# Hymba-style step on one core: first norm from token rows, x turned block by block, weight units at the head of the first pass

## What is computed

```
mod = (silu(c) @ ada_w + ada_b)             # 9 vectors of 2048 for each of 9 conditions
h = rmsnorm(x, g1) * (1 + sc1) + sh1        # rmsnorm: x * rsqrt(mean(x*x) + eps) * g
x = x + 0.5 * gt1 * (silu(h @ wg) * (h @ wu)) @ wd      # 2048 -> 5504 -> 2048
...                                         # mixer, second feed-forward, last norm
```

## Time and profile before

| | us |
|---|---|
| median of 3 runs | 2408.03 |
| lowest, highest | 2407.75, 2410.68 |
| the profiled execution | 2407.99 |
| its span, first to last instruction | 2405.5 |
| PE busy in the span | 2356.3 (98%) |
| DVE busy | 1202.7 (50%) |
| ACT busy | 838.0 (35%) |
| POOL busy | 151.1 (6%) |

### The profile page before, as it was taken

The page is one execution under the profiler, slowest core; times in us unless marked ns, Lnnn a source line. Parts: engine busy times, 40 slices in busy tenths (PEclk is TensorE's granted clock), DMA queues, the critical chain, the costliest instruction groups (busy, mean ns, idle before and its releaser), DMA issues.

```text
span 2405.5 us, 45693 instructions
## 1 busy us (share of the span) xinstructions
PE 2356.3 (98%) x17264; PEld 2258.3 (94%) x17264; DVE 1202.7 (50%) x2084; ACT 838.0 (35%) x1130; POOL 151.1 (6%) x176
## 2 busy tenths in 40 slices
PE   7999999999999999998999998999999999999998
PEld 3888999999999999998999898999999999999998
DVE  3665434434533454357676746454454454456344
ACT  3332222222222232334566634332333232333234
POOL 3000000000000000021031211000000000000003
PEclk9999999999999999999999999999999999999999
DMA  9999998889889948863444453554554555454553
GB/s 316 359 332 350 281 278 266 263 262 278 270 258 278 270 147 245 255 192 114 146 134 123 123 148 116 147 157 138 154 157 140 149 156 148 140 159 147 145 154 104
DMA packets 680252, 480.98 MB, mean 200 GB/s; under 512 B 15349, under 2 KB 603785, under 8 KB 679801
## 3 DMA queue, kind: packets, MB, share of 16 engines
q1 hardware_dynamic: 678224, 473.36, 65.8%
q0 software_dynamic: 1776, 6.26, 0.8%
q10 hardware_dynamic: 162, 0.14, 0.0%
HBM read 476.53 MB, written 5.13 MB: 200 GB/s over the span
## 4 chain that ended last, share of the span: by engine, by line
PE 91%; DVE 4%; ACT 2%; issue 1%; DMA 1%; DVEq 0%; ACTq 0%
PE ps L558 28%; PE ps L560 28%; PE ps L559 28%; PE ps L569 6%; PE ps L544 1%; DVE lo L1366 1%; DMA ident<-in_identity 0%; ACT hi L1021 0%; DMA mod_raw<-in_ada_w 0%; DVE work L1679 0%; DVE h_lo L1412 0%; DVE work L1725 0%; DVE work L1681 0%; DVE work L1401 0%; DVE work L1427 0%
## 5 line engine op out<-in xcount | busy, mean ns | idle before, releaser
L558 PE MATMUL ps<-h_hi,hi 128*128 128x320 f32 x3456 | 1079.0, 312 | 18.5 <-DVE h_lo L1412 11.8
L560 PE MATMUL ps<-h_hi,lo 128*128 128x320 f32 x3456 | 1070.5, 310 | 0.0
L559 PE MATMUL ps<-h_lo,hi 128*128 128x320 f32 x3456 | 1070.5, 310 | 0.0
L1366 DVE TENSOR_TENSOR lo<-raw,hi 128x1024 fp32r<-128x1024 f32 (+1 forms) x608 | 731.8, 1221 | 492.3 <-ACT hi L1021 491.1
L1021 ACT ACTIVATE hi<-raw 128x1024 fp32r<-128x1024 f32 (+1 forms) x608 | 624.9, 1050 | 1009.6 <-PE ps L560 875.9
L558 PEld LDWEIGHTS ps<-h_hi,hi 128*128 128x128 f32 x3456 | 651.3, 188 | 35.2 <-issue 28.4
L559 PEld LDWEIGHTS ps<-h_lo,hi 128*128 128x128 f32 x3456 | 651.4, 188 | 0.7
L560 PEld LDWEIGHTS ps<-h_hi,lo 128*128 128x128 f32 x3456 | 651.2, 188 | 0.0
L558 PE MATMUL ps<-a_hi,hi 128*128 128x320 f32 x1376 | 426.8, 310 | 1.3 <-DVE a_lo L1540 1.3
L560 PE MATMUL ps<-a_hi,lo 128*128 128x320 f32 x1376 | 425.2, 309 | 0.0
L559 PE MATMUL ps<-a_lo,hi 128*128 128x320 f32 x1376 | 425.1, 309 | 0.0
(11 more groups left out here) (221 smaller groups left out, 875.5 us busy)
## 6 DMA issues: line engine op xcount, KB each, us to landing
raw<-in_ffn_w_gate SPq DMA_DIRECT2D x172, 512.0 KB, 4.2
raw<-in_ffn_w_up SPq DMA_DIRECT2D x172, 512.0 KB, 5.1
raw<-in_ffn_w_down SPq DMA_DIRECT2D x160, 512.0 KB, 4.8
mod_raw<-in_ada_w SPq DMA_DIRECT2D x144, 512.0 KB, 7.8
work<-in_ada_w SPq DMA_DIRECT2D x144, 512.0 KB, 8.2
raw<-in_w_in SPq DMA_DIRECT2D x56, 512.0 KB, 3.8
raw<-in_w_out SPq DMA_DIRECT2D x32, 512.0 KB, 3.8
raw<-in_ffn_w_down SPq DMA_DIRECT2D x16, 384.0 KB, 2.9
```

Of the source, the lines that this page charges most:

```text
L558: mm(out, w_hi, r_hi, start=first, stop=False)
L559: mm(out, w_hi, r_lo, start=False, stop=False)
L560: return mm(out, w_lo, r_hi, start=False, stop=last)
L1366: v.tensor_tensor(lo_slot(u)[:, 0:n], raw_slot(u)[:, 0:n], hi_slot(u)[:, 0:n], ALU.subtract).then_inc(lo_done, 1)
```

## The change

It has four parts.

1. **First norm token by token.** The squares of the first norm are no longer taken from the turned blocks. ACT squares the three token tiles with a sum along the row (`accum_out`), makes rstd for each token by Ln and Exp on a 128x3 tile, DVE multiplies the identity by each of the three columns (`diag`), and PE multiplies ones by these three diagonals (`spread_rstd`), which lays rstd along the row on all partitions; ACT copies it out. POOL's 16 additions, the 16 squares on ACT and the sum by ones are gone; POOL's sample work for the first norm multiplies by rstd first, then by scale, then adds the shift.
2. **x turned one block per modulation unit.** Two blocks ahead, then one after each of the first 14 of the 16 units of groups 0 and 1. The parameters are turned after the seventh, `mod_turn(0)` after the ninth, `spread_rstd` after the tenth.
3. **Weight units first.** In the first quarter PE's order becomes unit 0, unit 1, group 2 parts 0 to 3, unit 2, unit 3, group 2 parts 4 to 7, unit 4, `mod_turn(2)`, unit 5, group 3 (all eight), unit 6, `mod_turn(3)`, unit 7. SP's order becomes units 0, 1, group 2 parts 0 to 3, units 2, 3, group 2 parts 4 to 7, units 4, 5, group 3 (all eight), units 6 to 9, group 4 parts 0 to 3, units 10, 11, and on.
4. **The identity first** in ACT's queue of transfers, ahead of c.

```
+TURN_AT = 2
+HALVES_0 = {2: ((2, 0),), 4: ((2, 4),), 6: ((3, 0), (3, 4))}
...
-            for u in range(4):
+            for u in range(8):
+                for group, first in HALVES_0.get(u, ()):
+                    head_group(group, range(first, first + 4))
                 head_unit(u)
-            head_group(2, range(MODS))
-            for u in range(4, 8):
+            for u in range(8, 10):
                 head_unit(u)
...
+            for h in range(4, 22):
+                head_group(2 + h // 2, range(h % 2 * 4, h % 2 * 4 + 4))
+                head_unit(2 * h + 2)
+                head_unit(2 * h + 3)
...
+            def spread_rstd():
+                pe.wait_ge(diag_ready, 1)
+                for t in range(3):
+                    n = P if t < 2 else SAMP
+                    last = mm(psum[:, 5, t * P:t * P + n], ones[0:n, :], diag[0:n, t, 0:n], start=True, stop=True)
+                last.then_inc(rstd_spread, 1)
 
             pe.wait_ge(x_in, 3 * 16)
+            for k in range(TURN_AT):
+                turn_x(k)
+            pe.wait_ge(c_ready, 1)
             for u in range(FIRST):
-                if u < MODS:
-                    turn_x(2 * u)
-                    turn_x(2 * u + 1)
-                if u == 0:
-                    pe.wait_ge(c_ready, 1)
                 mod_unit(u % MODS, u // MODS)
-                if u == MODS - 1:
+                if u + TURN_AT < KB:
+                    turn_x(u + TURN_AT)
+                if u == MODS - 2:
                     turn_parameters()
+                if u == MODS:
                     pe.wait_ge(prm_ready, 1)
                     mod_turn(0)
-                if u == SUM_AT:
-                    sum_of_squares(0)
+                if u == MODS + 1:
+                    spread_rstd()
             mod_turn(1)
...
                 for i in range(8):
-                    if i % 2 == 0:
+                    if q == 0:
+                        halves = HALVES_0.get(i, ())
+                    else:
+                        halves = ((first if i < 4 else second, i % 4 * 2),) if i % 2 == 0 else ()
+                    for group, part in halves:
                         for n in range(4):
-                            mod_unit(i % 4 * 2 + n, first if i < 4 else second)
+                            mod_unit(part + n, group)
                     quarter_unit(q, i)
-                    if i == 2:
+                    if i == (4 if q == 0 else 2):
                         mod_turn(first)
...
+            act.dma_start(ident[:, :], io['identity']).then_inc(ident_in, 16)
             act.dma_start(c_tok[0:1, :], io['c_prompt']).then_inc(c_in, 16)
             act.dma_start(c_tok[1:NC_, :], io['c_sample']).then_inc(c_in, 16)
-            act.dma_start(ident[:, :], io['identity']).then_inc(ident_in, 16)
...
-            for k in range(KB):
-                square(k, 0, dve_freed, k + 1)
+            act.wait_ge(x_in, 3 * 16)
+            squares = h_hi[:, :, :].rearrange("p k n -> p (k n)")
+            more = h_lo[:, :, :].rearrange("p k n -> p (k n)")
+            for t in range(2):
+                run(squares[:, t * D:(t + 1) * D], x_tok[:, t, :], ACT.Square, accum_out=ssq[:, t:t + 1])
+            chain(run(more[0:SAMP, 0:D], x_tok[0:SAMP, 2, :], ACT.Square, accum_out=ssq[0:SAMP, 2:3]))
+            chain(run(ssq, ssq, ACT.Ln, bias=eps, scale=1.0 / D))
+            run(ssq, ssq, ACT.Exp, scale=-0.5).then_inc(first_rstd, 1)
             copy_group(0)
+            act.wait_ge(rstd_spread, 1)
+            run(rstd, psum[:, 5, 0:T], ACT.Copy).then_inc(rstd_ready, 1)
             split(0)
...
-                    if i == 2:
+                    if i == (4 if q == 0 else 2):
                         copy_group(2 * q + 2)
...
-            parameters()
-            add_mod(0, 0)
+                if k == 7:
+                    parameters()
+                if k == 9:
+                    add_mod(0, 0)
+                    dve.wait_ge(first_rstd, 1)
+                    v.tensor_scalar(diag[:, 0, :], ident[:, :], ssq[:, 0:1], None, ALU.mult)
...
-            add_squares(0, KB)
-            samples(1, 0)
+            first_samples()
```

More of the change, by code:

```diff
@@ L101 @@
 SIDE_BY_SIDE = ((0, 0), (1, 0), (0, 1), (1, 1))
-SUM_AT = MODS + 1
-SUMMED = (0, KB, 2 * KB - 1, 3 * KB - 2)
-SET_UP = 2
+TURN_AT = 2
+HALVES_0 = {2: ((2, 0),), 4: ((2, 4),), 6: ((3, 0), (3, 4))}
+SUMMED = (0, 0, KB - 1, 2 * KB - 2)
+SET_UP = 3
 def mixer_plan():
@@ L216, in build @@
         sum_sq, at = carve(at, T)
+        diag, _ = carve(at - T, 3, P)
         sq, at = carve(at, 2, T)
@@ L280, in build @@
         sink_pick = small[:, 74:78]
+        ssq = small[:, 42:45]
         eps = small[:, 78:79]
@@ L477, in _ @@
             head_group(1, range(MODS))
-            for u in range(4):
+            for u in range(8):
+                for group, first in HALVES_0.get(u, ()):
+                    head_group(group, range(first, first + 4))
                 head_unit(u)
-            head_group(2, range(MODS))
-            for u in range(4, 8):
+            for u in range(8, 10):
                 head_unit(u)
[L483 to L492, removed]
+            for h in range(4, 22):
+                head_group(2 + h // 2, range(h % 2 * 4, h % 2 * 4 + 4))
+                head_unit(2 * h + 2)
+                head_unit(2 * h + 3)
+            for u in range(46, 48):
+                head_unit(u)
             head_group(13, range(MODS))
@@ L602, in sum_of_squares @@
             def sum_of_squares(n):
[L603 to L610, removed]
+                pe.wait_ge(summed, SUMMED[n] + KB - 1)
+                mm(psum[:, B_NORM, 0:T], ones, sum_sq, start=True, stop=False)
+                pe.wait_ge(squared, n * KB)
+                mm(psum[:, B_NORM, 0:T], ones, sq[:, (KB - 1) % 2, :], start=False, stop=True).then_inc(ms_ready, 1)
+            def spread_rstd():
[4 more added lines that the diff above has]
+                last.then_inc(rstd_spread, 1)
             pe.wait_ge(x_in, 3 * 16)
+            for k in range(TURN_AT):
+                turn_x(k)
+            pe.wait_ge(c_ready, 1)
             for u in range(FIRST):
-                if u < MODS:
-                    turn_x(2 * u)
-                    turn_x(2 * u + 1)
-                if u == 0:
-                    pe.wait_ge(c_ready, 1)
                 mod_unit(u % MODS, u // MODS)
-                if u == MODS - 1:
+                if u + TURN_AT < KB:
+                    turn_x(u + TURN_AT)
+                if u == MODS - 2:
                     turn_parameters()
+                if u == MODS:
                     pe.wait_ge(prm_ready, 1)
                     mod_turn(0)
-                if u == SUM_AT:
-                    sum_of_squares(0)
+                if u == MODS + 1:
+                    spread_rstd()
             mod_turn(1)
@@ L997, in _ @@
             token_sums(sum_sq, B_NORM)
-            pe.wait_ge(squared, 3 * KB + KB)
+            pe.wait_ge(squared, 3 * KB)
             token_sums(sq[:, (KB - 1) % 2, :], B_LAST)
@@ L1062, in copy_group @@
                 copy_mod()
-            for k in range(KB):
-                square(k, 0, dve_freed, k + 1)
+            act.wait_ge(x_in, 3 * 16)
[6 more added lines that the diff above has]
+            run(ssq, ssq, ACT.Exp, scale=-0.5).then_inc(first_rstd, 1)
             copy_group(0)
+            act.wait_ge(rstd_spread, 1)
+            run(rstd, psum[:, 5, 0:T], ACT.Copy).then_inc(rstd_ready, 1)
             split(0)
-            run(warm, eps, ACT.Ln)
-            act.wait_ge(ms_ready, 1)
-            chain(run(ln_ms, psum[:, B_NORM, 0:T], ACT.Ln, bias=eps, scale=1.0 / D))
             copy_group(1)
-            run(rstd, ln_ms, ACT.Exp, scale=-0.5).then_inc(rstd_ready, 1)
             modulate(0, 0, 0, Q)
@@ L1849, in _ @@
             g.memset(eps, EPS).then_inc(set_up, 1)
+            g.memset(ssq, 1.0).then_inc(set_up, 1)
             row = 0
@@ L1884, in add_squares @@
                 for m in range(end):
-                    pool.wait_ge(squared, n * KB + m + 1)
+                    pool.wait_ge(squared, (n - 1) * KB + m + 1)
                     if m == 0:
-                        if n:
-                            pool.wait_ge(ms_ready, n)
+                        if n > 1:
+                            pool.wait_ge(ms_ready, n - 1)
                         g.tensor_copy(sum_sq, sq[:, 0, :]).then_inc(summed, 1)
@@ L1902, in scaled_samples, with first_samples @@
                 return g.tensor_tensor(out, x[:, k:k + Q, SEQ:T].rearrange("p k (b s) -> p k b s", s=DS), vec(sc, k), ALU.mult)
-            def samples(sc, sh):
-                for q in range(4):
-                    pool.wait_ge(scale_ready, q + 1)
+            def first_samples():
+                pool.wait_ge(rstd_ready, 1)
+                for q in range(QUARTERS):
                     k = q * Q
                     out = h_samp[:, k:k + Q, :].rearrange("p k (b s) -> p k b s", s=DS)
[L1910 to L1913, removed]
```

(6 more changed lines are left out.)

12 lines of the change are left out of this document (8 added, 4 removed).

## The result

The changed kernel takes 2421.69 us in the median of 5 runs (2416.50 to 2423.47); the kernel before took 2409.69 in the same set (5 runs, 2407.75 to 2411.04). The ratio is 1.0046, with a 95% interval of 1.0035 to 1.0057: slower by 12.0 us. The profiled execution is the fastest of the five: 2416.5 us, span 2413.3, which is 7.8 above the span before.

A forecast was written before the change was run, and what follows sets the result against it. PE, busy 98% of the span, was taken to bound the kernel; head 3.4, queue stall 8.5, low clock 1.8 and second quarter 1.0 sum to +14.7 on 2408.03, so 2422.7 us, range 2412.5 to 2427.

The forecast's parts named there:

- SP's queue: Before unit 5: unit 6's transfer waits behind group 3; stall +8.5, low clock +1.8; again at the second quarter, +1.0.
- E: The end of group 2 on PE, from which the forecast counted transfer landings and the start of unit 5 (E + 12.5).
- the sum from the rows: Landing times from profiled transfers, 4.77 us for a first one and 1.42 each after: unit 7 at E + 10.5.
- Start: Kernel start: identity ahead of c makes c land at 12.1 and x begin at 15.85, +1.95.
- The bound of -1.0: Kernel start, the other bound: c still lands at 7.04 and PE waits only for x, first block at 12.9.
- c lands early: Rival at the start: identity and c both land by about 10 us; total 2419.7 us; chance 0.15.
- PE's work in the head: PE up to mod_turn(1): 0.93 and 1.37 removed, three matmuls as wide as a block's transposes added, 0.9.
- The clock: Head: PE stays at 1.2 GHz up to the end; last four modulation units +1.85, mod_turn(1) +0.25.
- the rival of the clock: Head: 2.4 GHz soon after x starts, unit 0 at 42.1; sum +2.9, 2410.9 us; chance 0.12.
- From mod_turn(1) to unit 0: Wait for the first h falls from 4.6 to 3.6 us, since rstd's multiplication now precedes the scale.
- rstd is long ready, so nothing takes its place: Wait before unit 0: nothing replaces the 0.99 us POOL operation taken from behind the scale.
- Head as a sum: All head terms, unit 0's low clock (+0.6) included: +3.4, or +0.4 with c early.

The follow-up runs named there:

- run 12: Changed kernel with only PE's turnings reordered: eight blocks of x first, then group 0's modulation units without transposes between; 2414.95 us, ratio 1.0024.
- run 9: Changed kernel with SP's whole order of the kernel before, and eight blocks of x turned before group 0's uninterrupted modulation units; 2403.25 us, ratio 0.9976.
- run 4: The changed kernel again, unaltered; 2421.99 us median of 4 runs, profiled execution 2422.07 us.
- run 7: Kernel before with only 14 spare matmuls on PE at its start; 2410.65 us, ratio 1.0004.
- run 10: As run 9, plus 10 spare matmuls on PE behind mod_turn(1), in the wait for the first h; 2401.99 us, ratio 0.9971.
- run 1: Changed kernel with only units 6 and 7 issued ahead of group 3's second half in SP's order; 2414.49 us, ratio 1.0018.
- run 5: Changed kernel with SP's order of the kernel before, plus 14 spare matmuls on PE while it waits for the identity; 2403.61 us, ratio 0.9984.
- run 6: As run 5, plus 10 spare matmuls on PE behind mod_turn(1); 2409.44 us, ratio 0.9989.
- run 8: Changed kernel with SP's order of the kernel before and c ahead of the identity again; one execution, 2404.59 us.
- run 11: Changed kernel with its third part undone wholly, plus run 9's order of turnings; 2405.93 us, ratio 0.9984.

## Why the prediction was right, step by step

The mechanism of the largest term was right, and its size nearly. The head was not: its total came out near by errors that cancel, which is luck.

- **SP's queue, right and nearly of the size.** Forecast: stall 8.5 and low clock 1.8 before and in unit 5, then 1.0. In the first profiled execution unit 5 starts at E + 11.8 where E + 3.95 would be undisturbed: 7.9. Between the fixed points the first two terms together measure 9.1 to 9.8 for 10.3, the last 1.6 to 2.1 for 1.0. With the clock alike, SP's order costs 11.7 (run 12 less run 9), for 11.3 forecast. The spacing of transfers was a little better than 1.42 us (unit 6 came 9.5 us after part 4 was issued, for 10.4). By the Trainium skill, page DMA: Bandwidth & Descriptors, section Anatomy of one DMA, unit 7 would have come at E + 7.8; it came at E + 9.8, nearer the sum from the rows.
- **Start, the wrong bound.** I took c to land at 12.1 behind the identity, and x to begin at 15.85. Silu begins at 8.54, and x, bound by its own transfer, at 13.96 (13.15 in run 4). The bound of -1.0 was the right one, with -0.7 to +0.1 measured. The rival "c lands early" was true, and its time, 2419.7, is further from the median than the forecast's.
- **PE's work in the head, too small.** `spread_rstd` takes 1.84 at 1.2 GHz, not 0.9: its three products are six matmul instructions where three transposes are three. Some 0.3 more: in the kernel before, the two units of 42.72 already took 1.70 for 2.02, so five units and not four were short there. And 0.2 is a wait for the first weights.
- **The clock, right in most executions.** "I let it stay at 1.2 GHz up to the end" is what run 4 shows, whose 2422.07 us is near both medians (2421.69 and 2421.99); six of the nine times lie from 2421.69 to 2424.03, but only one of these executions was profiled. In the first profiled one, of 2416.5 us, the clock rose at 35 us, part of the way to the rival of the clock, with the queue's stall still in it. I treated as one case what is different from one execution to the next. The Trainium skill, page TensorE: Matmul & The Clock Gate, section Part 4: PE-mode transpose, has transposes not count as a busy PE; the 24 transposes of run 9, low throughout, and the old mixture, low from 13 to 38 us in run 7, agree, but in the new one the clock rose at 23 to 35 us in five executions and not before the end of group 1 in three, and that the page does not decide.
- **From mod_turn(1) to unit 0, the gain that did not come.** Forecast 3.6 us for 4.6, since POOL has one operation less behind the scale. Measured 4.38 in both profiled executions of the changed kernel. POOL is early, but DVE is not:

```profile
45.44 0.69 POOL L1936 TENSOR_TENSOR work<-work,mod 128x256 f32<-128x256 f32 x1
46.09 0.90 POOL L1932 TENSOR_TENSOR work<-x,work 128x256 f32<-128x256 f32 x1
```
```profile
44.71 2.57 DVE L1414 SCALAR_TENSOR_TENSOR work<-x,mod,work 128x256 f32<-128x256 f32 x3
47.20 0.41 DVE L1421 TENSOR_TENSOR h_lo<-work,h_hi 128x256 fp32r<-128x256 f32 x1
```

  Three products on DVE take 2.57 us beside POOL (0.48 for the one at 48.26, without it), and the sample part of `h_lo` stands behind them. "rstd is long ready, so nothing takes its place" was the wrong sentence: DVE's own order took its place. The kernel before shows it on DVE, whose `h_lo` waited only 0.20 us for ACT's copy of POOL's result; so little could be gained there, however early POOL is:

```profile
48.94 2.12 DVE L1401 SCALAR_TENSOR_TENSOR work<-x,mod,work 128x256 f32<-128x256 f32 x3 [0.64 <-ACT work L1072]
51.27 0.43 DVE L1408 TENSOR_TENSOR h_lo<-work,h_hi 128x256 fp32r<-128x256 f32 x1 [0.20 <-ACT h_hi L1056]
```

- **Head as a sum**: +3.4 forecast. In run 4 unit 0 starts at 53.39; with group 2's 1.86 that is +2.3, and +0.7 for the low clock in unit 0: +3.0. The start taken 2.7 too late was nearly made up by work taken 1.4 too small and a gain taken 0.8 too large. In the first profiled execution it is -2.8 and nothing for the clock.
- **The whole sum, measured.** Run 4: 3.0 + 9.6 + 2.1 = 14.7, for a difference of spans of 14.6. First profiled execution: -2.8 + 9.1 + 1.6 = 7.9, for 7.8. Nothing is left over, so the change costs nothing outside these places.

## What to carry to other kernels

When a load is put behind another in a queue, ask what the other waits for, and whether the consumer of the first is due earlier than that: here a weight unit due after unit 2 was queued behind a slot freed after unit 3, and two engines stood still in order behind it. Take apart what an order change does on each engine's queue: PE's new order with SP's old one beats both kernels, while SP's order alone costs 11.7 us. Where the times of one kernel form two heaps, compare two fixed points that enclose the edit before judging it by its median; a difference of whole spans can hold a stretch of low clock a thousand us further on. And when a median moves as expected, look whether the mechanism did (run 10).

## What the runs showed of the hardware

- In one and the same stretch of alternating modulation units and transposes the clock rose at 23, 27, 29, 29 and 35 us in five executions and not before 48 us in three. Where this stretch stands, executions fall in heaps some 8 us apart (2406.6 and 2414.5 with units 6 and 7 moved), and the shares differ between kernels that are alike up to that point (10 of 11 in the lower heap with SP's old order, 2 of 11 with units 6 and 7 moved). Why they differ stays open.
- Behind 160 us the profiled executions keep their distances (in the median of ACT's instructions, to within 0.1 us) up to 1340 us and again behind 1400. Between lies a stretch of 3.4 us at the low clock near 1370 us, which runs 1, 5, 6, 7, 8 and 11 have and the others don't; it costs 1.5 us.
- The granted clock in the windows reads 1.00 from the start until its first change, also where modulation units take 1.08 us (20 to 30 us in the changed kernel); in run 5, where it had risen and fallen before, it reads 0.50 beside the same 1.08. In the head it has to be read from durations.
- Three transfers on ACT's queue, 72 KB of c and 64 KB of identity, have all landed by 7.8 to 8.5 us with the identity first, and by 10.9 to 12.1 with it last. I had assumed the last landing to be independent of the order; no run here tells the reason.
